# Two MoE and dense transformer blocks on one core: the experts' gate/up matmuls taken load by load through three token groups, and the later layers placed behind the experts' branch

## The reference, cut to what matters

```python
def moe_swiglu(h, router_w, router_b, w_gate, w_up, w_down):
    logits = jnp.einsum('bsd,de->bse', h, router_w) + router_b
    top_vals, top_idx = lax.top_k(logits, TOP_K)              # 2 of 8
    top_w = jax.nn.softmax(top_vals, axis=-1)
    combine = jnp.sum(jax.nn.one_hot(top_idx, N_EXPERTS) * top_w[..., None], axis=-2)
    y = jnp.zeros_like(h)
    for e in range(N_EXPERTS):
        y = y + combine[..., e:e + 1] * swiglu(h, w_gate[e], w_up[e], w_down[e])
    return y
def swiglu(h, w_gate, w_up, w_down):                          # hidden width 3584
    return (jax.nn.silu(h @ w_gate) * (h @ w_up)) @ w_down
```

## Time and profile before

| | us |
|---|---|
| median of three runs | 2715.02 (2713.2 to 2717.0) |
| the profiled execution, own time | 2720.17 |
| its span | 2718.4 |
| PE busy | 2639.1 (97%) |
| DVE busy | 1027.0 (38%) |
| ACT busy | 450.1 (17%) |
| mean granted PE clock | 0.987 of full speed |
| DMA, mean over the span | 235 GB/s |

### The profile page before, as it was taken

How to read it: one execution, slowest core, us unless ns; L and a number is a source line. 1 busy time by engine, 2 the same in 40 slices (tenths; PEclk the granted TensorE clock), 3 DMA queues, 4 the chain that set the end, 5 groups by cost and what they waited for, 6 DMA issues and landing times.

```text
span 2718.4 us, 42094 instructions
## 1 busy us (share of the span) xinstructions
PE 2639.1 (97%) x18832; PEld 1431.7 (53%) x18832; DVE 1027.0 (38%) x2083; ACT 450.1 (17%) x963; POOL 43.9 (2%) x74
## 2 busy tenths in 40 slices
PE   6999999999999999999989998999999999989998
PEld 4568647433433334334334445558886445554883
DVE  3533557311110111110212778746665422273034
ACT  1110011200000100000012534321110023332000
POOL 0000000101001001000000000000000000000000
PEclk9999999999999999999989999999999999989999
DMA  9879854599999999999962341024253341113541
GB/s 317 320 263 329 321 201 186 207 409 404 414 410 408 410 405 411 402 406 411 407 264 85 136 159 58 32 93 155 94 174 151 132 159 62 68 58 109 166 148 73
DMA packets 230884, 639.98 MB, mean 235 GB/s; under 512 B 14980, under 2 KB 97160, under 8 KB 205032
## 3 DMA queue, kind: packets, MB, share of 16 engines
q1 hardware_dynamic: 227624, 628.92, 60.9%
q0 software_dynamic: 2496, 6.19, 0.6%
q10 hardware_dynamic: 576, 2.10, 0.2%
HBM read 632.31 MB, written 6.95 MB: 235 GB/s over the span
## 4 chain that ended last, share of the span: by engine, by line
PE 84%; SPq 6%; DMA 4%; DVE 3%; ACT 1%; issue 1%; DVEq 0%; ACTq 0%
PE banks L1856 17%; PE banks L1664 9%; PE banks L1623 9%; PE banks L1743 8%; PE banks L1876 7%; PE banks L1326 6%; PE banks L1384 6%; SPq L797 4%; PE banks L1223 3%; PE banks L1590 3%; DMA sb_arena<-moe_w_up 2%; PE banks L1705 2%; PE banks L1183 2%; PE banks L956 1%; DMA sb_weights<-ada_w 1%
## 5 line engine op out<-in xcount | busy, mean ns | idle before, releaser
L1856 PE MATMUL banks<-sb_weights,sb_arena 128*32 128x512 f32 (+1 forms) x3840 | 372.9, 540 | 3.6 <-DMA sb_weights<-moe_w_up 3.4
L1856 PEld LDWEIGHTS banks<-sb_weights,sb_arena 128*32 128x32 f32 x3840 | 126.3, 110 | 238.8 <-issue 210.6
L1664 PE MATMUL banks<-sb_hT,sb_weights 128*128 128x256 f32 x1152 | 251.2, 380 | 0.4 <-ACT sb_arena L2291 0.4
L1664 PEld LDWEIGHTS banks<-sb_hT,sb_weights 128*128 128x128 f32 x1152 | 218.2, 190 | 33.2 <-issue 2.9
L3341 DVE TENSOR_TENSOR sb_hT<-sb_hT,banks 128x256 f32<-128x256 f32 (+1 forms) x96 | 53.0, 552 | 482.2 <-ACT sb_hT L2396 462.6
L1856 PE MATMUL banks<-sb_arena 128*32 128x512 f32 (+1 forms) x2304 | 229.8, 543 | 4.0 <-DMA sb_arena<-moe_w_up 4.0
L1743 PE MATMUL banks<-sb_weights,sb_arena 128*128 128x512 f32 x528 | 229.4, 594 | 1.5 <-ACT sb_gate_bc L2007 1.5
L1876 PE MATMUL banks<-sb_weights,sb_hT 128*32 128x512 f32 (+1 forms) x2240 | 182.6, 486 | 0.0
L1743 PEld LDWEIGHTS banks<-sb_weights,sb_arena 128*128 128x128 f32 x528 | 99.4, 190 | 125.8 <-issue 123.9
L2396 ACT ACTIVATE sb_hT<-banks 128x256 f32<-128x256 f32 (+1 forms) x96 | 34.3, 358 | 786.7 <-PE banks L1856 786.7
L1326 PE MATMUL banks<-sb_weights,sb_hT 128*128 128x512 f32 (+1 forms) x400 | 162.5, 564 | 1.4 <-ACT sb_mod_rows L2122 1.4
(11 more groups left out here) (374 smaller groups left out, 2808.4 us busy)
## 6 DMA issues: line engine op xcount, KB each, us to landing
sb_weights<-moe_w_gate SPq DMA_DIRECT2D x70, 1024.0 KB, 15.6
sb_weights<-moe_w_up SPq DMA_DIRECT2D x70, 1024.0 KB, 18.8
sb_weights<-moe_w_down SPq DMA_DIRECT2D x70, 1024.0 KB, 15.7
sb_weights<-w_mod SPq DMA_DIRECT2D x48, 1024.0 KB, 7.0
sb_weights<-w_ffn_in SPq DMA_DIRECT2D x44, 1024.0 KB, 7.7
sb_arena<-moe_w_gate SPq DMA_DIRECT2D x42, 1024.0 KB, 16.3
sb_arena<-moe_w_up SPq DMA_DIRECT2D x42, 1024.0 KB, 19.3
sb_arena<-moe_w_down SPq DMA_DIRECT2D x42, 1024.0 KB, 16.7
```

The costliest lines, as they stand in the source:

```text
L1664: mm = pe.matmul(dst, ring[j][:, k, lo:lo + P], hT[:, k, 0:T * P], start=(k == 0), stop=(k == KC - 1))
L1856: mm = pe.matmul(psum[32 * q:32 * q + 32, r % 2, 0:2 * w], ex_hT[:, half * GROUPS + g, k, :], wts[:, q, :, :, :], start=(k == 0), stop=(k ...
```

## The change

There are two parts. In the first, `gate_up` takes a piece `u` at once: for each k-chunk it runs all three groups before it goes to the next, so that a load is read by three groups in succession and then freed. The three groups of a piece stand in three PSUM banks, with six banks for two pieces (`expert_bank`); `turn_pick` moves from bank 7 to bank 2 and from behind round 2 to behind piece 0. ACT and DVE still work in 12 rounds; ACT now waits for DVE's product of two rounds before, and for the last two at an expert's end. `bring_back` and `add_back` keep their rounds. In the second, the code behind the experts becomes `after_experts()` on PE and DVE; it stands directly in the branch that is taken here (`over == 0`), and a second copy stands in the `Else` behind the further batches. SP and ACT keep their branch.

```diff
+        def expert_bank(u, g):
+            return (0, 1, 4, 5, 6, 7)[u % 2 * GROUPS + g]
...
-                    def gate_up(r):
-                        u, g, w = round_of(r)
-                        if r >= 2:
-                            pe.wait_ge(hb_done_e, c.up(hb_done_e))
+                    def gate_up(u):
+                        w = GU if u < 3 else P
+                        if u >= 2:
+                            pe.wait_ge(hb_done_e, c.up(hb_done_e, GROUPS))
                         for k in range(KC):
                             n = gu_load(u, k)
                             arrived(n)
...
-                            for q in range(4):
-                                mm = pe.matmul(psum[32 * q:32 * q + 32, r % 2, 0:2 * w],
...
-                            if g == GROUPS - 1:
+                            for g in range(GROUPS):
+                                for q in range(4):
+                                    mm = pe.matmul(psum[32 * q:32 * q + 32, expert_bank(u, g), 0:2 * w],
+                                                   ex_hT[:, half * GROUPS + g, k, :], wts[:, q, :, :, :],
+                                                   start=(k == 0), stop=(k == KC - 1))
...
                                 if k == KC - 1:
-                                    owed.append(freed[slot(n)])
-                                elif gu_load(u, k + 1) != n:
-                                    mm.then_inc(freed[slot(n)], 1)
-                        mm.then_inc(gu_done_e, 1)
+                                    mm.then_inc(gu_done_e, 1)
+                            if k == KC - 1:
+                                owed.append(freed[slot(n)])
+                            elif gu_load(u, k + 1) != n:
+                                mm.then_inc(freed[slot(n)], 1)
...
                         if s == 0:
-                            pe.wait_ge(hb_done_e, c.up(hb_done_e, 2))
+                            pe.wait_ge(hb_done_e, c.up(hb_done_e, 2 * GROUPS))
...
                     over = moe(0)
-                    with pe.If(over > 0):
+                    counts, taken, held = c.mark(), list(turns), list(owed)
+                    with pe.If(over == 0):
+                        after_experts()
+                    c.back_to(counts)
+                    turns[:], owed[:] = taken, held
+                    with pe.Else():
                         for batch in range(1, BATCHES):
                             moe(batch)
-                    turn_tile(2, 4, ctx_n[:, 0, :])
-                    scatter(last_scattered)
-                    tile_in()
-                    turn_tile(3, 4, ctx_n[:, 1, :])
-                else:
-                    ffn(L, T_OUT[L])
+                        after_experts()
...
                     for r in range(ROUNDS):
                         act.wait_ge(gu_done_e, c.up(gu_done_e))
-                        w = round_of(r)[2]
-                        act.activation(ex_sg[:, r % 2, 0:w], psum[:, r % 2, 0:w], ACT.Silu).then_inc(silu_done_e, 1)
+                        u, g, w = round_of(r)
+                        if r >= 2:
+                            act.wait_ge(hb_done_e, c.up(hb_done_e))
+                        act.activation(ex_sg[:, r % 2, 0:w], psum[:, expert_bank(u, g), 0:w], ACT.Silu).then_inc(silu_done_e, 1)
                         if last and r in (2, 4, 6, 8):
                             bring_back(r // 2 - 1)
+                    act.wait_ge(hb_done_e, c.up(hb_done_e, 2))
...
                     over = moe(0)
-                    with dve.If(over > 0):
+                    counts, load = c.mark(), list(last_load)
+                    with dve.If(over == 0):
+                        after_experts()
+                    c.back_to(counts)
+                    last_load[:] = load
+                    with dve.Else():
                         for batch in range(1, BATCHES):
                             moe(batch)
-                    dve.tensor_copy(st[:, 60:61], eps[:, :]).then_inc(last_y_copied, 1)
...
+                        after_experts()
```

More of the change, by code:

```diff
@@ L71, in at, with mark, back_to @@
         return now if self.it is None else self.it * self.per[s] + now
+    def mark(self):
+        return dict(self.n)
+    def back_to(self, mark):
+        self.n = dict(mark)
     def begin(self, it, *per):
@@ L1798, in turn_pick @@
                     for t in range(TX):
-                        tr = transpose(psum[:, 7, (2 * ab + t) * P:(2 * ab + t + 1) * P], pick_w[:, t, ab * P:(ab + 1) * P])
+                        tr = transpose(psum[:, 2, (2 * ab + t) * P:(2 * ab + t + 1) * P], pick_w[:, t, ab * P:(ab + 1) * P])
                 tr.then_inc(pick_turned, 1)
@@ L1889, in down @@
                             owed.append(freed[j])
-                    for r in range(ROUNDS):
-                        gate_up(r)
-                        if r == 0 and scatters:
+                    for u in range(4):
+                        gate_up(u)
+                        if u:
+                            continue
+                        if scatters:
                             scatter()
-                            c.up(y_added)
-                        elif r == 0 and not first:
+                            pe.wait_ge(y_added, c.up(y_added))
+                        elif not first:
                             pe.wait_ge(ex_y_copied, c.up(ex_y_copied))
-                        if r == 2 and (scatters or last):
-                            if scatters:
-                                pe.wait_ge(y_added, c.at(y_added))
+                        if scatters or last:
                             turn_pick()
@@ L1946, in _, with after_experts @@
             tile_in()
+            def after_experts():
+                turn_tile(2, 4, ctx_n[:, 0, :])
+                scatter(last_scattered)
+                tile_in()
+                turn_tile(3, 4, ctx_n[:, 1, :])
+                for L in stages:
+                    if L >= 2:
+                        out_proj(L, mixer2(L))
+                        ffn(L, T_OUT[L])
             for L in stages:
@@ L1949, in _ @@
                     out_proj1(L, mixer1(L))
-                else:
-                    out_proj(L, mixer2(L))
+                if L == 0:
+                    ffn(L, T_OUT[L])
                 if L == 1:
@@ L3339, in expert @@
                         dve.wait_ge(ff_ready_e, c.at(ff_ready_e))
-                        by_four = [v.rearrange("p (b c i) -> p b c i", c=GROUP, i=4) for v in (ex_sg[:, r % 2, 0:w], psum[:, r % 2, w:2 * w])]
+                        by_four = [v.rearrange("p (b c i) -> p b c i", c=GROUP, i=4) for v in (ex_sg[:, r % 2, 0:w], psum[:, expert_bank(u, g), w:2 * w])]
                         TT(ex_hb[:, r % 2, 0:w].rearrange("p (b i c) -> p b c i", c=GROUP, i=4), *by_four, ALU.mult).then_inc(hb_done_e, 1)
@@ L3408, in _, with after_experts @@
                 norm_copy(0, 0, t, (4, 1)[t])
+            def after_experts():
+                dve.tensor_copy(st[:, 60:61], eps[:, :]).then_inc(last_y_copied, 1)
+                norm_copy(2, 0, 2, 4)
+                for t in range(TX):
+                    add_scattered(t, last_scattered).then_inc(x_ready, 1)
+                    c.up(x_ready)
+                for t in range(TX):
+                    inverse(RS + t)
+                    STT(x[:, t, :], x[:, t, :], st[:, RS + t:RS + t + 1], final_gain, ALU.mult, ALU.mult)\
+                        .then_inc(x_ready, 1)
+                    c.up(x_ready)
+                    if t == 0:
+                        norm_copy(2, 0, 3, 4)
+                for t in range(TX):
+                    norm(t)
+                for t in range(TX):
+                    norm_copy(2, 0, t, 4)
+                for L in stages:
+                    if L >= 2:
+                        mixer2(L)
+                        ffn(L, T_OUT[L])
+                    if L == 2:
+                        for t in (2, 3):
+                            norm_copy(3, 0, t, 6)
             for L in stages:
@@ L3412, in _ @@
                     out_norm(L)
-                    if L:
-                        diagonal(diag_moe, L, 1, 0)
-                else:
-                    mixer2(L)
+                if L == 0:
+                    ffn(L, T_OUT[L])
                 if L == 1:
+                    diagonal(diag_moe, L, 1, 0)
                     dve.wait_ge(rest_in, REST)
```

32 lines of the change are left out of this document (4 added, 28 removed).

## The result

| | before | after |
|---|---|---|
| median of the comparison, us | 2715.1 (2708.54 to 2719.81, 6 runs) | 2699.43 (2697.92 to 2702.84, 6 runs) |
| ratio of times | | 0.994, 95% interval 0.9929 to 0.9951 |
| profiled execution, own time and span | 2720.17, 2718.4 | 2701.39, 2698.7 |
| PE busy | 2639.1 | 2626.2 |
| mean granted PE clock | 0.987 | 0.992 |

The change makes the kernel faster by 15.7 us between the medians, 0.6%. The forecast was 2698, inside a range of 2688 to 2711. The two profiled executions lie 18.8 us apart; against them the forecast was 17.4. The path splits into four pieces, with P the end of the last expert matmul. Each of these float32 matmuls shows as two rows in the trace: an expert's 12 rounds hold 12 x 8 x 4 = 384 gate/up matmuls, and their piece of the chain counts x768.

The account below looks back on a forecast made before the run. PE was taken to bound most of the experts' stretch, DMA almost as tight, with jump idles and slow clock behind. Terms -12.0 + 5.4 - 11.8 + 1.0 = -17.4 us gave 2698 us against the 2715.0 median; range 2688 to 2711.

Parts of the forecast that it names:

- The experts' weights: Experts' stretch: freeing loads earlier stops DMA being late, recovering 12.0 of the 12.7 us PE loses to weight waits and slow clock.
- The last expert: Between down(0) and down(1): serial transfers back make PE wait 3.7 us, plus 1.7 us of slow clock; +5.4 us.
- Behind the experts: After the last expert matmul: no jump idle, full clock, 40 layer-2 matmuls done sooner; 13.5 less 1.7, taken as 11.8 us gained.
- the second context tile's columns follow ... so PE waits 2.0 us: Layer 2's start: columns ready at P + 11.9, PE done with the first tile at P + 9.9; 1.7 us charged for clock.
- The end: After DVE's last instruction: jumping over the second copy passes the span's end by 0.9 us, taken as +1; bounds 0 and 1.3.
- The slower rival: Gate/up: changing group and bank every four matmuls causes short idles and clock drops in 32 pieces; +54 us, 2752; chance 0.05.
- The sum: Whole kernel: -12.0 + 5.4 - 11.8 + 1.0 = -17.4 us.

## Why the prediction was right

The total and its sign were right, the mechanisms came as described, and one term was mis-sized; that the two parts add up as forecast was in part luck (last point).

- **The experts' weights, -12.0.** Right. Slots are freed from 524.97 us (forecast 524.2), and the 7.4 us of waits for moe_w_up and their clock are gone. Working without a stall takes 866.5 us; with the 4.3 us, the 0.2 us and 1.6 us of clock that is 872.6, and 873.4 were measured. Undoing the early freeing alone brought 6.0 us of waits back and made the stretch 9.3 us longer.
- **The last expert, +5.4.** Right in mechanism, its place and its size: 4.3 us of wait (forecast 3.7; the two landings took 9.18 and 8.43 us, not twice 8.6) and 1.6 us of clock (1.7). Moving the transfers forward took both away.
- **Behind the experts, -11.8.** The branch does what was said, P + 24.0 with no idle row, but the gain in the profile is 15.1 us. The step that failed is "the second context tile's columns follow ... so PE waits 2.0 us", and with it the 1.7 us charged for the clock. I took eight rows of the trace for a tile's eight matmuls. Each of these float32 matmuls shows as two rows: a tile is the piece of 6.87 us with x16, and the 40 are two and a half tiles, not the five that I named ahead of the prediction. So the second tile is wanted 6.87 us behind 1399.77, at 1406.6, when its columns had been ready since 1405.17. Without wait and charge my sum would have been P + 23.6 and 13.5 + 2.0 = 15.5.
- **The end, +1.0.** Right in size (0.9), but its cause is only half shown. The Trainium skill's "Runtime: NRT & Kernel Launch" (Instruction fetch mechanics) says that a taken branch to a target that wasn't fetched ahead stalls. Every profile with the old jump agrees, with an idle row of 4.36 to 4.42 us on PE, and no profile with the branch turned round has that row. For the end, the run without the second copy agrees (1.8 us outside the span instead of 2.4 to 2.7). But the runs with 36 and with 16 more copies on DVE have the same jump and 1.75 to 1.88 us; and of the 11 runs with shifted code, which has no jump at the end, three showed 2.7 to 3.0. So the jump at the end need not cost the microsecond; what decides it stays open.
- **The slower rival** (short idles by changing banks) didn't come: a row of gate/up takes 592 ns, and the clock left 1.00 in the experts' stretch only behind the 4.3 us stall. The Trainium skill's "TensorE: Matmul & The Clock Gate" (A second HAM failure mode: psum-queue depth-cycling) has no counterpart in this trace.
- **The sum.** In the profile -18.8 against -17.4: the term behind the experts gave 3.3 us more, the start and the rest took 1.1 us back, and the experts 0.8 us. The medians moved by 15.7. The parts alone gave 0.54 and 0.37% on one chip and 0.6% together, so they don't add up; with the repeat of the first part, 0.34 and 0.37%, they would within their intervals. The order, worth -6.6 by the forecast, gave 14.0 and 10.5 us alone: in both of its profiles the 40 matmuls end at P + 29.9 without the branch, behind one idle row and a short slow clock. The branch, worth -10.8 with its microsecond at the end, gave 9.4 us alone and, on top of the order, 6.4 us in the medians on one chip. In the profiles it gave 5.9 us there (P + 24.0 against P + 29.9), and the rest, which I had moving along unchanged, took 1281.2 and 1281.8 us with both parts against 1275.9 and 1276.1 with the first alone: the two pairs of spans, 2698.7 and 2696.4 against 2698.9 and 2698.5, are nearly alike.

## What to carry to other kernels

When a ring of buffers feeds an engine that is nearly as slow as its DMAs, look first at when the slots come free early on: here the matmuls' order was worth 12 us in the experts' stretch, with the first freed slot 10 us sooner and DMA at 407 to 408 GB/s behind that with either order. Whatever then becomes ready in a bunch meets the next serial chain, so list what stands in the same queue (here two transfers through one buffer, on which DVE waits with finished rounds behind it); moving two of them and the last addition was worth another 5 us, at the bound of what can be told. Before pricing a wait by counting rows, set a row with a known amount of work beside the code, to see how many instructions one operation shows as.

## What the runs showed of the hardware that was not expected

- An idle of 4.3 or 7.9 us on PE cost 1.6 to 2 us of slow clock in two kernels: by windows the clock was back at 1.00 about 3 to 4 us after PE worked again, as in both profiles of the first part alone behind its jump of 4.4 us. In the two profiles of the kernel before, in the one with shifted code and in the one with 16 copies it took 13 to 15 us, although the idle with 16 copies was the shortest, 3.18 us. What ends the slow stretch wasn't settled. Over executions of one kernel the time goes with the mean clock: the kernel before spread over 11 us in 11 runs at clocks of 0.987 to 0.993, the change over 2.8 us in five at 0.991 and 0.992.
- The old jump on PE cost 4.4 us in all five profiles that have it, and a second 3.3 us two transposes later for one place of the target (two profiles) and none for two others (three profiles).
- From the 40 matmuls to the end of the span the same work took 1275.9 to 1283.9 us over fourteen profiles. By windows of 10 us, the slow clock costs 7.2 to 16.8 us there and PE isn't busy for 34.3 to 38.1; without both, 1232.3 to 1234.8 us are left in every profile. Why the two differ from kernel to kernel stays open. What is saved at the experts is thus not quite what the end sees: earlier transfers gained 5.4 us at the 40 matmuls, and 3.7 us of span.
